# Token columns of a projection unit: 512 + 512 + 128 along the PSUM banks in place of three times 384

## What is computed

```python
# layer 0: even mixer                      # layer 1: mLSTM mixer
z = rmsnorm(x) @ w_in                       z = rmsnorm(x) @ w_in
o = windowed attention(q, k, v, sink)       q, k = silu(causal conv width 4)
c = silu(layernorm(dwconv31(glu)))          h = chunked mLSTM(q, k, v, gates)
x = x + concat(o, c) @ w_out                x = x + (rms(h) * sigmoid(o)) @ w_out

def sq_relu_ffn(x, g, w1, w2):              # after either mixer, hidden 4096
    h = jax.nn.relu(rmsnorm(x, g) @ w1)
    return (h * h) @ w2
```

## Time and profile before

| | |
|---|---|
| three runs | 3057.49, 3059.36 (median), 3063.40 us |
| profiled execution, first to last instruction | 3060.3 us |
| TensorE matmul busy | 2824.8 us, 92%, 15623 matmuls |
| TensorE weight loads busy | 2715.7 us, 89%, 15623 loads |
| VectorE busy | 1298.9 us, 42% |
| GpSimd busy | 938.9 us, 31% |
| ScalarE busy | 510.5 us, 17% |
| mean granted TensorE clock | 0.957 |

### The profile page before, as it was taken

The page is one execution under the profiler, slowest core; times in us unless marked ns, Lnnn a source line. Parts: engine busy times, 40 slices in busy tenths (PEclk is TensorE's granted clock), DMA queues, the critical chain, the costliest instruction groups (busy, mean ns, idle before and its releaser), DMA issues.

```text
span 3060.3 us, 39793 instructions
## 1 busy us (share of the span) xinstructions
PE 2824.8 (92%) x15623; PEld 2715.7 (89%) x15623; DVE 1298.9 (42%) x1643; ACT 510.5 (17%) x877; POOL 938.9 (31%) x676
## 2 busy tenths in 40 slices
PE   7756798999999999999899999998999999999995
PEld 6755577999999999999888888888999999999995
DVE  7999865432222222226745444554432122212225
ACT  3000253211001100113131313131211001100111
POOL 2687900222222222222212122224222222222221
PEclk9888588999999999999899999999999999999998
DMA  4110002111111111112223232224111111111111
GB/s 147 31 31 15 14 13 76 41 35 43 41 41 44 44 41 41 41 42 102 46 46 81 51 81 46 80 61 142 42 42 41 41 41 41 41 41 41 41 42 62
DMA packets 92428, 155.59 MB, mean 51 GB/s; under 512 B 49608, under 2 KB 52680, under 8 KB 91576
## 3 DMA queue, kind: packets, MB, share of 16 engines
q1 hardware_dynamic: 27504, 100.15, 11.6%
q10 hardware_dynamic: 64568, 53.24, 5.7%
q0 software_dynamic: 272, 0.98, 0.1%
HBM read 129.94 MB, written 24.40 MB: 50 GB/s over the span
## 4 chain that ended last, share of the span: by engine, by line
PE 80%; DVE 10%; issue 7%; ACT 2%; DVEq 1%; ACTq 0%; DMA 0%; POOL 0%
PE psum L504 66%; PE psum L771 4%; PE psum L666 1%; PE psum L815 1%; PE psum L626 1%; PE psum L845 1%; PE psum L851 1%; DVE low L1002 1%; PE psum L805 1%; DVE h_lo L944 1%; DVE mid L941 1%; DVE high L1011 1%; DVE low L999 1%; ACT mid L1468 1%; PE psum L644 1%
## 5 line engine op out<-in xcount | busy, mean ns | idle before, releaser
L369 POOL TENSOR_SCALAR w_hi<-w_raw 128x1024 fp32r<-128x1024 f32 x191 | 208.5, 1091 | 1746.6 <-PE psum L504 1573.3
L504 PE MATMUL psum<-a_hi,w_hi 128*128 128x384 f32 x2808 | 653.7, 341 | 74.9 <-DVE mid L926 37.6
L504 PE MATMUL psum<-a_lo,w_hi 128*128 128x384 f32 x2808 | 646.1, 338 | 0.0
L504 PE MATMUL psum<-a_hi,w_lo 128*128 128x384 f32 x2808 | 644.0, 337 | 0.0
L504 PEld LDWEIGHTS psum<-a_hi,w_hi 128*128 128x128 f32 x2808 | 507.8, 191 | 81.2 <-DVE mid L926 38.6
L504 PEld LDWEIGHTS psum<-a_lo,w_hi 128*128 128x128 f32 x2808 | 509.2, 191 | 0.0
L504 PEld LDWEIGHTS psum<-a_hi,w_lo 128*128 128x128 f32 x2808 | 506.9, 190 | 0.0
L933 DVE TENSOR_TENSOR low<-psum,low 128x1152 f32<-128x1152 f32 x144 | 195.5, 1358 | 668.1 <-PE psum L504 668.1
L372 POOL TENSOR_TENSOR w_lo<-w_raw,w_hi 128x1024 fp32r<-128x1024 f32 x191 | 460.6, 2411 | 15.9
L504 PE MATMUL psum<-h_hi,w_hi 128*128 128x384 f32 x1536 | 355.9, 340 | 6.6 <-DVE h_lo L944 6.6
L504 PE MATMUL psum<-h_lo,w_hi 128*128 128x384 f32 x1536 | 354.3, 339 | 0.0
(11 more groups left out here) (216 smaller groups left out, 2526.4 us busy)
## 6 DMA issues: line engine op xcount, KB each, us to landing
w_raw<-in_wall SPq DMA_DIRECT2D x191, 512.0 KB, 3.5
low<-in_x ACTq DMA_DIRECT2D x16, 576.0 KB, 8.2
high<-in_mem_in ACTq DMA_DIRECT2D x32, 257.0 KB, 3.9
out_mem_s<-high ACTq DMA_DIRECT2D x32, 257.0 KB, 3.1
out_x_spill<-low ACTq DMA_DIRECT2D x8, 576.0 KB, 2.7
low<-out_x_spill ACTq DMA_DIRECT2D x8, 576.0 KB, 7.8
out_y<-low ACTq DMA_DIRECT2D x8, 576.0 KB, 2.9
out_mix_spill<-mid ACTq DMA_DIRECT2D x3, 1152.0 KB, 5.9
```

Source lines behind the costliest of these rows:

```text
L369: nc.gpsimd.tensor_scalar(w_hi[:, s, :], w_raw[:, s, :], 1.0, 1.0, ALU.mult, ALU.mult)\
L504: r = mm(psum[:, z + i, 0:TN], w[:, s, k * P:(k + 1) * P], a[:, kk, tok(i)], start=first and n == 0, stop=last and n == 2)
```

## The change

The pieces of a unit follow the PSUM banks: columns 0 to 511 and 512 to 1023 fill a bank each, the last 128 (the sample tokens) go into the third. A block's 1152 columns are then contiguous in PSUM, so `out3` is one run and `by3` does nothing. `qk_ext` needs one instruction for all 1024 prompt tokens where it needed two. NT and TN stay for the root-mean-square sums, the rotary products, the layer norm and the pieces of L771.

```diff
+BANKS = [(0, 512), (512, 1024), (1024, T)]
...
         def out3(b):
             s = 3 * (b % 2)
-            return psum[:, s:s + 3, 0:TN]
+            return psum[:, s:s + 3, :].rearrange("p a b -> p (a b)")[:, 0:T]

         def by3(v):
-            return v.rearrange("p (a b) -> p a b", a=NT)
+            return v
...
-                    for i in range(NT):
-                        r = mm(psum[:, z + i, 0:TN], w[:, s, k * P:(k + 1) * P], a[:, kk, tok(i)],
+                    for i, (t0, t1) in enumerate(BANKS):
+                        r = mm(psum[:, z + i, 0:t1 - t0], w[:, s, k * P:(k + 1) * P], a[:, kk, t0:t1],
                                start=first and n == 0, stop=last and n == 2)
...
-                    V.tensor_tensor(e[:, QH:QH + 2 * TN].rearrange("p (a b) -> p a b", a=2), z[:, 0:2, :],
-                                    by3(rbc[:, :])[:, 0:2, :], ALU.mult)
-                    V.tensor_tensor(e[:, QH + 2 * TN:QH + TP], z[:, 2, 0:TP - 2 * TN], rbc[:, 2 * TN:TP], ALU.mult)
-                    V.tensor_tensor(sample(e[:, QH + TP:QEXT], QH, QH + TB), sample(z[:, 2, TP - 2 * TN:TN], 0, TB),
+                    V.tensor_tensor(e[:, QH:QH + TP], z[:, 0:TP], rbc[:, 0:TP], ALU.mult)
+                    V.tensor_tensor(sample(e[:, QH + TP:QEXT], QH, QH + TB), sample(z[:, TP:T], 0, TB),
                                     sample(rbc[:, TP:T], 0, TB), ALU.mult).then_inc(evicted, 1)
```

## The result

The change makes the kernel slower: 3253.64 us median of 4 runs (3251.2 to 3255.45) against 3058.43 us (4 runs, 3051.03 to 3063.4), ratio 1.063, 95% interval 1.0617 to 1.0643. The forecast was 3230 us, +171; measured are +195.

The account below looks back on a forecast made before the run. TensorE was taken as the bound, through L504's matmuls after the input stage. Terms 112.8 + 64.5 - 6.1 - 0.6 = +170.6 us on 3059.4 gave 3230 us, range 3120 to 3700.

Parts of the forecast that it names:

- What bounds, and which triples are exposed: L504's matmul triples: 312 hidden beside VectorE in the input stage, 2496 + 1536 = 4032 exposed at full difference.
- The narrow slot: 128-column matmul in L504: the next weights' load shows, 112 ns as in L785; ends 55.8 and 224 ns.
- The wide slots: 512-column matmuls in L504: 226.8 ns each on a_hi/a_lo, 213.3 + 16.7 on h_hi/h_lo; bounds 215.8 and 231.3.
- I take it as one price per matmul with a load beside it: L504 at full clock: extra over the stream, 13.5 ns (a) or 16.7 ns (h), fixed per matmul.
- What comes back at the chunk's turn: FFN chunk, up to down half: 9 longer triples fill TensorE's wait for h_lo, 16 x 0.38 = -6.1 us.
- The gate stage: Gates and first head units: four L504 units counted as exposed, +4.3 us.
- VectorE's edits: Evictions unchanged at 1.36 us; `qk_ext` in one 1.22 us instruction, 0.15 us less, four heads, -0.6 us.
- A 128 slot costs what a 384 slot costs: Rival on L504: a load beside a full-rate stream sets 173.5 ns; +324 us, 3384 us, chance 0.12.
- the fp32 rate: Rival on L504: fp32r on 128 columns runs at fp32 rate, slot 224 ns; +622 us, 3681 us, chance 0.22.
- R of the experiments: Later theory on the narrow slot: fp32r under 256 columns streams at two cycles a column, 106.7 ns for 128.
- Nothing changes: Rival on L504: load under the short matmul fetched early enough, triple stays 520.4 ns; 3059 us, chance 0.07.
- The clock falls: Rival on TensorE's granted clock: a tenth of FFN triples at half clock, +121 us; 3351 us, chance 0.04.

## Why the prediction was right, point by point

- **What bounds, and which triples are exposed.** Right. TensorE's larger time shows outside the input stage in full; inside it nothing does (-1.8 us), with TensorE's busy time between 60 and 215 us up to 119.6 from 107.5 and VectorE's still 151:

```profile
60.00:215.00 155.00, 119.60 (x594) 99.68 (x592) 151.07 (x123) 3.50 (x3) 116.29 (x74) 0.90 0.12 32
```

- **The narrow slot.** Right in mechanism and nearly in size: 112 ns forecast (from L785, whose own stream of 106.7 ns may set its step), 108 measured, which is the bare load of the earlier trace rows. 64, 128 and 192 columns take the same 108, 256 take 117 to 121. By the Trainium skill, "TensorE: Matmul & The Clock Gate", section "LDWEIGHTS (loading the stationary operand)", a load takes its columns over 1.2 GHz: 107 ns for 128, an estimate. The trace agrees, with 108.
- **The wide slots.** This is the mis-sized term. The step "I take it as one price per matmul with a load beside it" failed: the extra is 10 ns at 256 columns and up to 24 at 512, and half a load takes at most 1.4 ns off. On a_hi/a_lo the 512 slots are 235.8 and 232.8 ns where 226.8 was forecast, even past the upper bound of 231.3, so a triple costs 13.81/24 = 575.4 ns in the unit above and 577 in the mean of all, +55 to +57 instead of +45.2. In 2424 such triples (the forecast's 2496 less three gate units, see below) that is +24 to +28 us of the miss. On h_hi/h_lo a triple is 572.2 against 529.2, +43.0 instead of +42.0: +2 us. These are net figures: two wide slots are 15.0 ns (a) and 3.9 ns (h) over the forecast, the narrow one 3.7 under it.
- **What comes back at the chunk's turn.** Right: the 0.43 us of idle are gone, in 16 chunks 6.6 us down to 0.2, where 6.1 were forecast. 96 x 55.0 + 96 x 43.0 = 9.4 us or somewhat more would have been added to a chunk, 9.2 were.
- **The gate stage.** Forecast +4.3 us for its four units, measured -4.1. Not all were exposed: after the first, TensorE's units lie beside a chain of row operations on VectorE, which sets the end. That chain became shorter, since GpSimd's weight split now falls elsewhere. Before, and then after (timelines of VectorE and GpSimd in that stage):

```profile
1460.25 1.49 DVE L1229 COPY high<-high 4x1152 f32<-4x1152 f32 x1
1461.78 2.25 DVE L1231 TENSOR_TENSOR high<-high,cols 4x8 f32<-4x8 f32 x1
...
1459.54 1.59 POOL L369 TENSOR_SCALAR w_hi<-w_raw 128x1024 fp32r<-128x1024 f32 x1 [8.76 <-issue]
1461.22 2.77 POOL L372 TENSOR_TENSOR w_lo<-w_raw,w_hi 128x1024 fp32r<-128x1024 f32 x1
```

```profile
1543.88 0.75 DVE L1230 COPY high<-high 4x1152 f32<-4x1152 f32 x1
1544.66 0.16 DVE L1232 TENSOR_TENSOR high<-high,cols 4x8 f32<-4x8 f32 x1
...
1546.22 2.35 POOL L370 TENSOR_SCALAR w_hi<-w_raw 128x1024 fp32r<-128x1024 f32 x1 [10.22 <-issue]
```

  The same two instructions take 3.74 us while GpSimd splits weights and 0.91 us when it does not, and the second ends with GpSimd's (1464.03 and 1463.99). A second such pair in this stage goes from 2.10 and 2.80 us to 1.35 and 0.75. Less one that became 0.66 us longer, the chain is 5.0 us shorter; with 1.3 us for the first unit that makes -3.7 of the measured -4.1. All 13 traces agree: of their 26 copies of 4x1152, 13 take 0.75 us, with GpSimd busy beside them for at most 0.17 us, and 13 take 1.49 to 2.84 us, with it busy for 1.4 us or more. No run moved GpSimd's work alone.
- **VectorE's edits.** Right: 1224 ns for the new instruction (1.22 forecast), evictions unchanged.
- **Rivals.** "A 128 slot costs what a 384 slot costs" (173.5) and "the fp32 rate" as it was priced (224) fell with 108 ns. At half that price, R of the experiments, the fp32 rate would have given 107 ns and the forecast's total by another mechanism; the prediction did not see this case, and only 192 columns at 108 ns and the halved load exclude it. "Nothing changes" fell too, and with it the 131 ns that the Trainium skill, "TensorE: Matmul & The Clock Gate", section "Back-to-back issue gap", gives for 512 columns: here a 512 slot takes 229 to 237 ns on average. "The clock falls" did not come: 0.961 against 0.957.

Together: of the 21.6 us between forecast and measured span difference (170.6 and 192.2), the table gives +19.9 to the FFNs, +8.2 to the heads, +4.4 to the output projections and +0.4 to the end, against -8.4 for the gates and -2.9 for the input stage and attention. Of the first three, 26 to 30 us are the triples; the few that are left, mostly in the heads, were not traced one by one. So the mechanism was right, but that the total came within 24 us is in part luck: the wide slots were priced some 42 us too low, the narrow slot 15 and the gate stage 8 too high. The chance of 0.22 on the fp32 rate, which drew the range up to 3700, was caution without a row for it.

## What to carry to other kernels

Where every matmul brings its own weights, as here, its time is the larger of its stream (with its extra) and the next load. Look for two load starts right after a wait: their distance is the bare load, 0.11 us for 128 weight columns here, worth some 260 moving columns at full rate. Cut the moving side so that no piece falls under that; an even cut at 384 loses nothing to a neat one at bank borders, and 384 + 512 + 256 has both the borders and the cover.

## What the runs showed of the hardware that was not expected

At the full clock an fp32r matmul costs more than its columns: 10 to 14 ns over the stream at 256, 13 to 17 at 320, 13 to 17 at 384, 20 to 22 at 448, 16 to 24 at 512 (means of slots in six placements). It does not grow with the length of the load beside it (ratio 0.9994 with half of it), it is absent at half clock and next to absent for fp32, and it changes with how the pieces are placed (the same widths mirrored: 0.9987 and 1.0048 of the kernel before) and from pass to pass. What makes it stays open.

A record can mislead about such a slot: a matmul whose weights are late opens its record before they are in, so that by matmul starts the wide slot seems to be 283 ns and the narrow one 60.
